# Half of the tokens by gathered expert rows, and GpSimd making lo parts: one encoder layer on one core

## The chip, the cores and the metric

The kernel runs on one core of a Trainium2 chip. The core has TensorE (PE, matrix products into PSUM), VectorE (DVE), ScalarE (ACT), GpSimd (POOL) and SyncE (SP, which here only issues DMAs). The metric is device microseconds of the program; the median of three runs counts. A profile is one more execution, taken by the hardware profiler.

## The reference, cut to what matters

One encoder layer on 1024 tokens of width 1024. The first half of it (gated linear attention, pooling, an output projection) is the same in both kernels. The second half is a product-key mixture of 16384 single-neuron experts:

```python
q = (ht @ w_q).reshape(T, 8, 2, 128)                       # 8 heads, two halves
s = einsum('thpd,hpnd->thpn', q, sub_keys)                 # 128 scores a half
vals, idx = top_k(s, 16)                                   # 16 best of each half
cand = vals[:, :, 0, :, None] + vals[:, :, 1, None, :]     # 256 sums
top_s, top_pos = top_k(cand.reshape(T, 8, 256), 16)        # 16 best sums: the chosen experts
gates = softmax(top_s)
a = gelu(einsum('td,ted->te', x, u_tab[experts]))          # 128 experts a token
y = einsum('te,ted->td', gates * a, v_tab[experts])
```

## The kernel before, in words

**Arithmetic.** Products in float32r keep float32's exactness by splitting each operand into a rounded part (`hi`, made by ScalarE, `split_hi`) and the rest (`lo`, a subtraction, `split_lo`). A product is then three matmuls: hi·hi, hi·lo, lo·hi. A "row" of experts is 128 x 1024 values (512 KB), and there are 128 such rows of u and of v.

**Tokens.** The 1024 tokens are 8 tiles of 128. Six are dense: the activation of every expert is computed and multiplied with a gate that is zero for the experts not chosen. Two are sparse (`SPARSE = 2`): for each of a token's 128 chosen experts GpSimd gathers the activation (`picked_act`, 4 bytes a token) and the row of v (`v_rows`, 4 KB a token) by indirect DMA, and VectorE adds the row, scaled, to a sum (`add_row`).

**Sweep 1** (`expert_sweep_1`) goes over the 128 rows of u. For each, TensorE makes 48 matmuls of 512 columns (8 slices of the width, 3 products, 2 halves of the tokens), ScalarE takes the gelu, and it goes to DRAM. Beside it VectorE finds the experts of the tokens, head by head (`topk_head`), and builds one-hot matrices of the chosen sub-keys by comparisons (`compare`, L1479); GpSimd multiplies these with the gates (L1393); and TensorE turns 8 tokens at a time into dense gates (L1555), which ScalarE copies and VectorE completes (L1492). VectorE also makes `u_lo` (L83).

**Sweep 2** (`expert_sweep_2`) goes twice over the 128 rows of v, three dense tiles a round (L1881: 18 matmuls a row and round). For each row VectorE multiplies gates and activations (`cf`, L1762), makes `c_lo` and `v_lo` (L83) and adds one gathered row (L1784). GpSimd issues the gathers in blocks of eight activations (L1668) and then eight rows (L1676), a row only when the sum that used its buffer is done.

The order on each engine is the order of the code; semaphores join the engines. TensorE's own loops are short, and each engine waits where its operands are not there.

Of the kernel before, what the change touches and what calls it, by code (L numbers as in the profile page):

```python
# [28 lines left out]
P = 128  # L29
D = 1024  # L30
# [18 lines left out]
TOK = 16  # L49
GTOK = P // 2  # L50
BLOCK_STEPS = GTOK // TOK
LOWEST = -3.0e38
SPARSE = 2
DENSE = TT - SPARSE
DTOK = DENSE * P
CHOSEN = HEADS * TOPK
TILE_STEPS = HEADS + 1
STEPS = NKEYS // 2
assert DENSE * TILE_STEPS + HEADS + 2 == STEPS
# [44 lines left out]
def layer(nc, t_in, out):  # L104
    g = Layer(nc, t_in, out)
    with ExitStack() as ctx:
# [44 lines left out]
        expert_sweep_1(g)  # L151
        expert_sweep_2(g)
# [856 lines left out]
def topk_buffers(g):  # L1009
    g.s_work = g.at("s_work", 96, [P, 2, NKEYS])  # L1010
    g.s_rest = g.at("s_rest", 97, [P, 2, NKEYS])
    g.cand = g.at("cand", 98, [P, TOPK, TOPK])
    g.cand_rest = g.at("cand_rest", 99, [P, TOPK, TOPK])
    g.match = g.at("match", 100, [P, 2, TOPK, TOPK])
    g.chosen = g.at("chosen", 102, [P, 2, HEADS, TOPK])
    g.top_all = g.at("top_all", 103, [P, HEADS, TOPK])
    g.vals = g.at("vals", 103.5, [P, 2, TOPK])
    g.tops = g.at("tops", 103.625, [P, TOPK])
    g.idx = g.at("idx", 103.6875, [P, 2, TOPK], U32)
    g.pos = g.at("pos", 103.8125, [P, TOPK], U32)  # L1020
    g.hilo = g.at("hilo", 103.875, [P, 2, TOPK], U32)
    g.gates = g.at("gates", 192, [P, HEADS, TOPK])
    g.norm = g.at("norm", 192.5, [P, HEADS])
    g.gate_hi = g.at("gate_hi", 194.75, [P, P], F32R)
    g.slots = g.at("slots", 192.75, [P, 4, P])


def topk_head(g, dve, h, topk_done):

    flat = lambda a: a.rearrange("p a b -> p (a b)")  # L1030
    for p in range(2):
        dve.max(g.vals[:, p, 0:8], g.s_work[:, p, :])
    dve.drain()
    for p in range(2):
        dve.max_index(g.idx[:, p, 0:8], g.vals[:, p, 0:8], g.s_work[:, p, :])
        dve.match_replace(g.s_rest[:, p, :], g.vals[:, p, 0:8], g.s_work[:, p, :], LOWEST)
# [4 lines left out]
    for p in range(2):  # L1041
        dve.max_index(g.idx[:, p, 8:16], g.vals[:, p, 8:16], g.s_rest[:, p, :])
# [912 lines left out]
```

## Time and profile before

| | us |
|---|---|
| runs (3) | 3346.50, 3348.01, 3355.24; median 3348.01 |
| profiled execution | 3326.69, its span 3324.8 |
| TensorE busy | 3126.2 (94% of the span), mean clock 0.978 |
| VectorE, ScalarE, GpSimd busy | 2256.7, 1017.1, 982.8 |
| HBM | 505.76 MB read, 134.22 MB written |

The span runs from the first instruction to the last. "Busy" of TensorE counts a matmul from start to its modelled end, so the pace of matmuls is read from their starts. The clock is what was granted, 1.00 being 2.4 GHz.

### The profile page before, as it was taken

How to read it: one execution, taken by the hardware profiler on the slowest of the kernel's cores; microseconds unless marked ns; L12 is line 12 of the kernel's file. 1: busy time of each engine (PE TensorE's matmuls, PEld its weight loads, DVE VectorE, ACT ScalarE, POOL GpSimd, SP SyncE). 2: the span in 40 equal slices, each digit the busy share in tenths (PEclk: the TensorE clock that was granted, in tenths of full speed). 3: DMA queues.
4: the chain of work that ended last, by engine and by line, in shares of the span. 5: the costliest groups of instructions: out<-in, count | busy, mean ns of one | idle time of the engine just before them, and what ended most of it. 6: DMA issues, size and time to landing. Idle time of an engine off the chain costs nothing. (4 is left out here: it accounts for less than half of the span.)

```text
span 3324.8 us, 44749 instructions
## 1 busy us (share of the span) xinstructions
PE 3126.2 (94%) x14706; PEld 2587.2 (78%) x14706; DVE 2256.7 (68%) x3986; ACT 1017.1 (31%) x1301; POOL 982.8 (30%) x727
## 2 busy tenths in 40 slices
PE   3993799989999999999999999999989998999996
PEld 3881587878888888888888888878878886788885
DVE  6345643568767677675876754438878888888886
ACT  3123453112232222322222221123333334333333
POOL 0000100013223233232332320026554557655541
PEclk9995899999999999999999999999999999999998
DMA  6410122223333423333233432249999999999995
GB/s 239 184 52 8 53 101 100 81 74 120 114 149 139 155 88 150 137 150 138 100 143 144 150 137 106 101 160 375 348 365 331 361 344 332 379 347 363 345 362 186
DMA packets 251408, 640.90 MB, mean 193 GB/s; under 512 B 28752, under 2 KB 134352, under 8 KB 249680
## 3 DMA queue, kind: packets, MB, share of 16 engines
q1 hardware_dynamic: 205568, 503.07, 41.2%
q0 software_dynamic: 45776, 137.00, 11.0%
q8 instruction: 37, 0.61, 0.1%
q14 instruction: 27, 0.22, 0.0%
HBM read 505.76 MB, written 134.22 MB: 192 GB/s over the span
## 5 line engine op out<-in xcount | busy, mean ns | idle before, releaser
L1393 POOL TENSOR_TENSOR onehot<-onehot,slots 128x1024 fp32r<-128x1024 f32 x192 | 369.1, 1944 | 1177.3 <-DVE onehot L1479 1177.3
L93 PE MATMUL acc_u<-a_hi,u_hi 128*128 128x512 f32 x2048 | 633.2, 390 | 2.5 <-PEq L1114 2.5
L93 PE MATMUL acc_u<-a_lo,u_hi 128*128 128x512 f32 x2048 | 631.2, 389 | 0.0
L93 PE MATMUL acc_u<-a_hi,u_lo 128*128 128x512 f32 x2048 | 630.8, 389 | 0.0
L1881 PE MATMUL y_ps<-v_hi,c_hi 128*128 128x512 f32 x1536 | 476.0, 391 | 31.4 <-DVE c_lo L83 29.1
L1881 PE MATMUL y_ps<-v_lo,c_hi 128*128 128x512 f32 x1536 | 474.6, 390 | 0.0
L1881 PE MATMUL y_ps<-v_hi,c_lo 128*128 128x512 f32 x1536 | 474.1, 390 | 0.0
L78 ACT ACTIVATE v_hi<-v_raw 128x1024 fp32r<-128x1024 f32 x256 | 271.5, 1061 | 649.1 <-PE y_ps L1881 619.1
L93 PEld LDWEIGHTS acc_u<-a_lo,u_hi 128*128 128x128 f32 x2048 | 384.6, 188 | 81.2
L93 PEld LDWEIGHTS acc_u<-a_hi,u_lo 128*128 128x128 f32 x2048 | 384.4, 188 | 80.5
L1415 ACT ACTIVATE gelu<-acc_u 128x1024 f32<-128x1024 f32 x128 | 131.5, 1027 | 1012.3 <-PE acc_u L93 1012.3
L93 PEld LDWEIGHTS acc_u<-a_hi,u_hi 128*128 128x128 f32 x2048 | 378.1, 188 | 75.2 <-issue 2.6
L83 DVE TENSOR_TENSOR v_lo<-v_raw,v_hi 128x1024 fp32r<-128x1024 f32 x256 | 314.4, 1228 | 172.1 <-ACT v_hi L78 171.7
L1676 POOL DMA_INDIRECT v_rows<-in_v,eidx x256 | 272.7, 1065 | 376.8 <-DVE y_part L1784 336.0
L1881 PEld LDWEIGHTS y_ps<-v_hi,c_hi 128*128 128x128 f32 x1536 | 288.1, 189 | 97.3 <-DVE v_lo L83 33.3
L1881 PEld LDWEIGHTS y_ps<-v_hi,c_lo 128*128 128x128 f32 x1536 | 289.1, 188 | 60.6
L1881 PEld LDWEIGHTS y_ps<-v_lo,c_hi 128*128 128x128 f32 x1536 | 289.1, 188 | 60.5
L1784 DVE SCALAR_TENSOR_TENSOR y_part<-v_rows,coef,y_part 128x1024 f32<-128x1024 f32 x256 | 331.4, 1297 | 0.1
L1668 POOL DMA_INDIRECT picked_act<-act_d,aidx x256 | 304.0, 1187 | 77.9 <-issue 77.9
L83 DVE TENSOR_TENSOR u_lo<-u_raw,u_hi 128x1024 fp32r<-128x1024 f32 x128 | 165.4, 1292 | 207.2 <-ACT u_hi L78 207.2
L1492 DVE TENSOR_TENSOR gate_block<-gate_block,gate_ps 128x1024 f32 (+1 forms) x96 | 116.7, 1216 | 214.4 <-ACT gate_block L1426 214.4
L1479 DVE TENSOR_TENSOR onehot<-consts,slots 128x1024 fp32r<-128x1024 f32 x192 | 239.4, 1288 | 0.9 <-issue 0.9
(227 smaller groups left out, 3403.9 us busy)
## 6 DMA issues: line engine op xcount, KB each, us to landing
v_raw<-in_v SPq DMA_DIRECT2D x256, 512.0 KB, 7.5
u_raw<-in_u SPq DMA_DIRECT2D x128, 512.0 KB, 4.2
act_d<-gelu SPq DMA_DIRECT2D x128, 512.0 KB, 2.6
gate_d<-gate_block SPq DMA_DIRECT2D x12, 4096.0 KB, 12.1
gt<-gate_d SPq DMA_DIRECT2D x64, 768.0 KB, 7.8
at<-act_d SPq DMA_DIRECT2D x256, 192.0 KB, 6.1
w_mod_b<-in_w_mod SPq DMA_DIRECT2D x6, 2560.0 KB, 9.0
w_mod<-in_w_mod SPq DMA_DIRECT2D x9, 1024.0 KB, 16.4
```

The lines of the kernel that those rows point to most:

```text
L78: return act.activation(hi, raw, ACT.Copy)
L83: return dve.tensor_tensor(lo, raw, hi.bitcast(F32), ALU.subtract)
L93: done = pe.matmul(acc[:, cols], w, a[:, k, cols], start=first, stop=last)
L1393: last_op = pool.tensor_tensor(onehot_2[u][:, :, part, :], onehot_2[u][:, :, 0, :].bitcast(F32), gate.unsqueeze(2).to_broadcast([P, TOK // ...
L1415: act.activation(gelu[s][:], acc[s][:], ACT.Gelu).then_inc(gelu_done, 1)
L1479: last = dve.tensor_tensor(rows, g.iota.unsqueeze(1).to_broadcast([P, TOK // 2, NKEYS]), chosen.unsqueeze(2).to_broadcast([P, TOK // 2, NK ...
L1492: dve.tensor_tensor(dst, dst, gate_psum(1), ALU.add).then_inc(gate_out, 1)
L1668: pool.indirect_dma_start(out=picked_act[:, e:e + 1], out_offset=None, in_=act_table, in_offset=bass.IndirectOffsetOnAxis(ap=index(g.aidx, ...
L1676: pool.indirect_dma_start(out=rows[e % UNROLL][:], out_offset=None, in_=v_table, in_offset=bass.IndirectOffsetOnAxis(ap=index(g.eidx, e), ...
L1784: dve.scalar_tensor_tensor(sums, rows[k][:], coef[:, k:k + 1], sums, ALU.mult, ALU.add).then_inc(rows_done, 1)
L1881: done = pe.matmul(yps[t][:, cols], c, v[s][:, cols], start=first and k == 0, stop=last and k == 2)
```

## The change

`SPARSE` goes from 2 to 4: four tiles are dense and four gathered. The experts' part becomes one program of three passes with one ring of four buffers for rows of u and v:

- pass 1: all rows of u against the sparse half of the tokens (24 matmuls a row). In it the retrieval and the dense gates are made, one head and eight tokens for each two rows. GpSimd makes `u_lo`.
- pass 2: all rows of u once more, against the dense half. VectorE makes `u_lo`. The gathers begin here: `rows_after` says how many rows are to be added after each row of experts, 7 for 3 rows, 284 in this pass.
- pass 3: all rows of v once, all four dense tiles (24 matmuls a row), with 23 gathered rows for 12 rows of experts, 228 in this pass. `cf`, `c_hi` and `c_lo` are made for two rows of experts at once, in one buffer of 128 x 1024.

Retrieval takes 112 candidate sums in place of 256 (with both lists sorted, the other 144 cannot be among the best 16), made by two small additions, and finds the experts of four heads at once (`decode_half`). The number of heads for which this is done in the experts' part stays 57. All engines' programs but TensorE's are written out without loops. GpSimd's gathers now alternate, one row and one activation, eight rows of either ahead. Dense gates are stored in blocks of 32 tokens in place of 64.

```diff
-SPARSE = 2
+WIDE = 4
+CANDS = WIDE * TOPK + (TOPK - WIDE) * WIDE
+SPARSE = 4
+GATE_TOK = 8
+ORDER = (1, 4, 2, 5, 3, 6, 7)
+FIRST_ROWS = 5
+def rows_after(x):
+    in_sweep_1 = max(0, min(x, 2 * HALF // 8 - 1) - FIRST_ROWS) * 7 // 3
+    return min(SPARSE * CHOSEN, in_sweep_1 + max(0, x - (2 * HALF // 8 - 1)) * 23 // 12)
...
+def half_product(pe, acc, w_hi, w_lo, a_hi, a_lo, half):
+    cols = slice(half * HALF, (half + 1) * HALF)
+    for k in range(KC):
+        wh, wl = w_hi[:, k * P:(k + 1) * P], w_lo[:, k * P:(k + 1) * P]
+        pe.matmul(acc, wh, a_hi[:, k, cols], start=k == 0, stop=False)
+        pe.matmul(acc, wh, a_lo[:, k, cols], start=False, stop=False)
+        done = pe.matmul(acc, wl, a_hi[:, k, cols], start=False, stop=k == KC - 1)
...
+            for p in range(U // 2):                                  # GpSimd, pass 1
+                split(2 * p + 2)
+                split(2 * p + 3)
+                if p:
+                    weigh(p - 1)
+            weigh(U // 2 - 1)
...
+            for r in range(BATCH):
+                pick_act(r)
...
+            for r in range(SPARSE * CHOSEN):                         # GpSimd, passes 2 and 3
+                fetch_row(r)
+                if r + BATCH < SPARSE * CHOSEN:
+                    pick_act(r + BATCH)
...
+            for p in range(U // 2):                                  # VectorE, pass 1
+                if p == 1:
+                    close(0)
...
+                    topk_head(g, dve, h, g.s_work[p % 2], topk_read)
+                    if h % HALF_HEADS == HALF_HEADS - 1:
+                        decode_half(g, dve, h // HALF_HEADS, g.chosen[n % 2])
...
+                    compare(p - 1)
+                if p >= 2:
+                    gates_low(p - 2)
...
+                for half in range(2):                                # VectorE, pass 2
+                    split(e + 2 + half)
+                    upto = rows_after(2 * p + half)
+                    for r in range(done, upto):
+                        add_row(r)
...
+            for m in range(N_STEPS):                                 # VectorE, pass 3
+                if m % 2 == 0 and m + 2 < N_STEPS:
+                    combined(m // 2 + 1)
+                if m + 2 < N_STEPS:
+                    split(V + m + 2)
+                upto = rows_after(U + m)
+                for r in range(done, upto):
+                    add_row(r)
...
+                if m % 2 == 0 and m + 2 < N_STEPS:
+                    combined_low(m // 2 + 1)
```

GpSimd in the u sweep, before: one step of 16 tokens, four multiplications with the gates and no lo part (`onehot_3592` and `onehot_3593` are the two buffers of one-hot matrices).

```order
L1393 TENSOR_TENSOR onehot_3592<-onehot_3592,slots 128x8x128
L1393 ISA
L1393 TENSOR_TENSOR onehot_3592<-onehot_3592,slots 128x8x128
L1389 REGISTER_ALU
L1393 ISA
L1393 TENSOR_TENSOR onehot_3593<-onehot_3593,slots 128x8x128
L1393 ISA
L1393 TENSOR_TENSOR onehot_3593<-onehot_3593,slots 128x8x128
```

In pass 1 of the changed kernel, two pairs of rows of u:

```order
L99 TENSOR_TENSOR u_lo_3799<-u_raw_3795,u_hi_3797 128x1024
L99 TENSOR_TENSOR u_lo_3800<-u_raw_3796,u_hi_3798 128x1024
L1457 TENSOR_TENSOR onehot_3804<-onehot_3804,slots 128x8x128 x2
L99 TENSOR_TENSOR u_lo_3057<-u_raw_3053,u_hi_3055 128x1024
L99 TENSOR_TENSOR u_lo_3058<-u_raw_3054,u_hi_3056 128x1024
L1457 TENSOR_TENSOR onehot_3803<-onehot_3803,slots 128x8x128 x2
```

Each pair of rows now puts two subtractions and two multiplications in GpSimd's queue.

VectorE in the u sweep, before, from the middle of one head's retrieval to the end of its step:

```order
L1043 TENSOR_TENSOR cand<-vals 128x256
L1047 MAX tops<-cand 128x8
L1049 MAX_INDEX pos<-tops,cand 128x8
L1050 MATCH_REPLACE cand_rest<-tops,cand 128x256
L1052 MAX tops<-cand_rest 128x8
L1054 MAX_INDEX pos<-tops,cand_rest 128x8
L1055 ISA
L1055 COPY top_all<-tops 128x16
L1058 TENSOR_SCALAR hilo<-pos 128x16
L1059 TENSOR_SCALAR hilo<-pos 128x16
L1062 TENSOR_TENSOR match<-hilo,consts 128x512
L1065 TENSOR_TENSOR match<-match,idx 128x512
```

In pass 1 of the changed kernel the same stretch, up to the next head:

```order
L1061 TENSOR_TENSOR cand<-vals 128x64
L1064 TENSOR_TENSOR cand<-vals 128x48
L1069 MAX top_all<-cand 128x8
L1071 MAX_INDEX pos<-top_all,cand 128x8
L1072 MATCH_REPLACE cand_rest<-top_all,cand 128x112
L1074 MAX top_all<-cand_rest 128x8
L1076 MAX_INDEX pos<-top_all,cand_rest 128x8
L1611 TENSOR_TENSOR onehot_3801<-consts,slots 128x1024
L1611 TENSOR_TENSOR onehot_3803<-consts,slots 128x8x128
L1618 TENSOR_TENSOR gate_block_3805<-gate_block_3805,ps 128x128x8
```

The one addition has become two next to each other, and the search for the experts has left the head's step.

GpSimd's gathers, before: a block of eight activations, and rows (`v_rows_7646` and so on are the eight buffers).

```order
L1668 DMA picked_act<-act_d,aidx 128x1 x8
L1676 DMA v_rows_7646<-in_v,eidx 128x1024
L1676 DMA v_rows_7647<-in_v,eidx 128x1024
L1676 DMA v_rows_7648<-in_v,eidx 128x1024
L1676 DMA v_rows_7649<-in_v,eidx 128x1024
```

And in the changed kernel:

```order
L1487 DMA v_rows_3816<-in_v,eidx 128x1024
L1479 DMA picked_act<-act_s,aidx 128x1
L1487 DMA v_rows_3817<-in_v,eidx 128x1024
L1479 DMA picked_act<-act_s,aidx 128x1
L1487 DMA v_rows_3818<-in_v,eidx 128x1024
```

There are still two gathers for each row of v, now one behind the other, and twice as many in all.

## Rows read from the trace of the kernel before

**Rows 1.** Stages: start:end, length, PE, PEld, DVE, ACT, POOL busy (count), clock, DMA share, GB/s.

```profile
520.00:700.00 180.00, 179.70 (x906) 152.66 (x905) 82.39 (x229) 30.61 (x31) 0.00 (x0) 1.00 0.27 91
743.00:2200.00 1457.00, 1453.25 (x6761) 1217.04 (x6762) 976.70 (x2177) 388.66 (x385) 359.69 (x188) 1.00 0.35 130
2221.00:2740.00 519.00, 507.56 (x2221) 419.66 (x2222) 410.48 (x503) 183.01 (x247) 286.40 (x262) 0.98 0.95 349
3298.00:3325.00 27.00, 0.97 (x5) 0.47 (x3) 10.75 (x11) 5.33 (x12) 5.83 (x4) 0.59 0.24 97
```

**Rows 2.** First matmuls of the u sweep, by tile (duration min/median/max; first, last start).

```profile
L93 PE MATMUL acc_u<-a_hi,u_hi x2048: 389/389/628, 716.5 to 2213.0; 128*128 128x512 f32 x187
```

**Rows 3.** PE in order of time, 1007 to 1020 us (start, duration, what).

```profile
1007.52 1.12 PE L1555 MATMUL gate_ps<-onehot,onehot 128*128 128x256 f32 x8
1008.47 0.63 PE L93 MATMUL acc_u<-a_hi,u_hi 128*128 128x512 f32 x2
...
1019.38 1.12 PE L1555 MATMUL gate_ps<-onehot,onehot 128*128 128x256 f32 x8
```

**Rows 4.** VectorE in order of time from 717 us, GpSimd idle.

```profile
717.27 0.49 DVE L1032 MAX8 vals<-s_work 128x8 f32<-128x128 f32 x2
...
720.14 0.41 DVE L1043 TENSOR_TENSOR cand<-vals 128x256 f32<-128x256 f32 x1
...
725.46 0.69 DVE L1067 TENSOR_REDUCE chosen<-match 128x32 f32<-128x512 f32 x1
```

**Rows 5.** VectorE in order of time, 1017 to 1028 us.

```profile
1017.32 1.43 DVE L1043 TENSOR_TENSOR cand<-vals 128x256 f32<-128x256 f32 x1
1018.82 0.43 DVE L1047 MAX8 tops<-cand 128x8 f32<-128x256 f32 x1
...
1021.19 0.16 DVE L1055 COPY top_all<-tops 128x16 f32 x1
...
1023.96 1.21 DVE L1492 TENSOR_TENSOR gate_block<-gate_block,gate_ps 128x1024 f32 x1
...
1026.23 2.35 DVE L1479 TENSOR_TENSOR onehot<-consts,slots 128x1024 fp32r<-128x1024 f32 x2
```

**Rows 6.** GpSimd over the same stretch.

```profile
1014.71 3.76 POOL L1393 TENSOR_TENSOR onehot<-onehot,slots 128x1024 fp32r<-128x1024 f32 x2 [5.89 <-DVE onehot L1479]
```

**Rows 7.** VectorE, the same operation without and with a GpSimd operation beside it.

```profile
401.15 1.23 DVE L83 TENSOR_TENSOR wo_lo<-wo_raw,wo_hi 128x1024 fp32r<-128x1024 f32 x1 [2.55 <-ACT wo_hi L78]
...
403.49 2.20 DVE L83 TENSOR_TENSOR wo_lo<-wo_raw,wo_hi 128x1024 fp32r<-128x1024 f32 x1
```

**Rows 8.** GpSimd there, and its add in the tail.

```profile
402.15 12.48 POOL L83 TENSOR_TENSOR a_lo<-z,a_hi 128x1024 fp32r<-128x1024 f32 x4 [85.19 <-ACT a_hi L78]
...
3312.08 2.33 POOL L1683 TENSOR_TENSOR y<-y,x 128x1024 f32<-128x1024 f32 x1 [5.68 <-DVE y L1796]
```

**Rows 9.** Groups by line, sweep 2 (count, busy us, mean ns, idle before).

```profile
L1784 DVE SCALAR_TENSOR_TENSOR y_part<-v_rows,coef,y_part 128x1024 f32<-128x1024 f32 x256 | 331.4, 1297 | 0.1
...
L1668 POOL DMA_INDIRECT picked_act<-act_d,aidx x256 | 304.0, 1187 | 77.9 <-issue 77.9
...
L1676 POOL DMA_INDIRECT v_rows<-in_v,eidx x256 | 272.7, 1065 | 376.8 <-DVE y_part L1784 336.0 <-issue 40.8
```

**Rows 10.** GpSimd gathers in order of time at 2318 us.

```profile
2318.32 1.67 POOL L1668 DMA_INDIRECT picked_act<-act_d,aidx  x1 [0.30 <-issue]
2320.29 1.36 POOL L1668 DMA_INDIRECT picked_act<-act_d,aidx  x1 [0.30 <-issue]
2321.95 0.94 POOL L1668 DMA_INDIRECT picked_act<-act_d,aidx  x1 [0.30 <-issue]
```

**Rows 11.** VectorE over the same stretch.

```profile
2319.08 0.55 DVE L83 TENSOR_TENSOR c_lo<-cf,c_hi 128x384 fp32r<-128x384 f32 x1
...
2320.74 0.55 DVE L1762 TENSOR_TENSOR cf<-gt,at 128x384 f32<-128x384 f32 x1
2322.07 1.23 DVE L83 TENSOR_TENSOR v_lo<-v_raw,v_hi 128x1024 fp32r<-128x1024 f32 x1 [0.78 <-ACT v_hi L78]
```

More of the change, by code:

```diff
@@ L1020, in topk_buffers @@
[L1020 to L1030, printed above, removed]
+    g.s_work = [g.at(f"s_work{s}", 88 + s, [P, 2, NKEYS]) for s in range(2)]
+    g.match = g.at("match", 90, [P, 2, HALF_HEADS * TOPK, TOPK])
@@ new lines, in fetch_row @@
+            def fetch_row(r):
+                if r >= ROWS:
+                    pool.wait_ge(rows_done, r - ROWS + 1)
+                pool.indirect_dma_start(out=rows[r % ROWS][:], out_offset=None, in_=v_table,
+                                        in_offset=bass.IndirectOffsetOnAxis(ap=index(g.eidx, r), axis=0))\
+                    .then_inc(rows_in[r % ROWS], 16)
+            pool.wait_ge(aidx_ready, 1)
+            for s in range(2):
+                pool.wait_ge(act_stored[s], U // 2 * 16)
@@ new lines, in gates, with pair @@
+            def gates(b, u, first=False):
+                pe.wait_ge(onehot_ready, b + 1)
+                if not first:
+                    pe.wait_ge(gate_out, b)
+                for t in range(GATE_TOK):
+                    last = pe.matmul(gps[:, t], onehot_1[u][:, t, :], onehot_2[u][:, t], start=True, stop=True)
+                last.then_inc(gate_ps, 1)
+            def pair(p, odd, half=1, first_gates=False, slots=None):
+                e = 2 * p
+                pe.wait_ge(lo_pool, e + 1)
+                product(e, 2 * odd, 1)
+                gates(p - 2, odd, first_gates)
+                if slots is not None:
+                    transpose_slots(slots)
+                pe.wait_ge(lo_pool, e + 2)
+                product(e + 1, 2 * odd + 1, 1)
@@ new lines, in _ @@
+            for e in range(4):
+                pe.wait_ge(lo_pool, e + 1)
+                product(e, e, 1, e >= 2)
+                if e == 2:
+                    transpose_slots(0)
+            pair(2, 0, first_gates=True)
+            pair(3, 1)
+            for j in range(DENSE):
+                first = TILE_GATES * j + (4 if j == 0 else 2)
+                with pe.Fori(first // 2, TILE_GATES * (j + 1) // 2) as q:
+                    pair(2 * q, 0)
+                    pair(2 * q + 1, 1)
+                if j + 1 < DENSE:
+                    pair(TILE_GATES * (j + 1), 0)
+                    pair(TILE_GATES * (j + 1) + 1, 1, slots=j + 1)
@@ L1901, in lay_out @@
+            for s in range(RING):
+                m = N_STEPS - RING + s
+                if s % 2 == 0:
+                    pe.wait_ge(clo_r, m // 2 + 1)
+                combine(V + m, s, last=s == RING - 1)
 def lay_out(a):
```

1063 lines of the change are left out of this document (482 added, 581 removed).

## The prediction

> **What bounds the kernel now.** I read the stages first, then each engine in order of time. In the u sweep TensorE is busy for 1453.25 of 1457 us, in a round of the v sweep for 507.56 of 519 [rows 1]: its matmuls set the time. The sweep's first matmul starts at 716.5 us [rows 2]. 48 matmuls lie between 1008.47 and 1019.38: 10.91 us, 0.227 us each; eight gate matmuls take 0.95 us [rows 3]. VectorE and GpSimd have room, but the DMA engines in the v sweep show a share of 0.95 at 349 GB/s.
>
> **How VectorE and GpSimd meet.** An addition of two 256-element inputs takes 0.41 us alone and 1.43 us when it is issued inside two GpSimd operations that run from 1014.71 to 1018.47; it ends at 1018.75 [rows 4 to 6]. A VectorE subtraction of 1.23 us takes 2.20 us in the 12.48 us in which GpSimd makes four subtractions (3.12 us each, 2.33 us for one with less beside it) [rows 7, 8]. So an operation of one with both inputs in SBUF waits for the other's to end, and they take turns. The gathers show it too: the one issued at 2318.32 takes 1.67 us and the next VectorE operation starts at 2319.08; that of 2320.29 takes 1.36, VectorE's next starts at 2320.74; that of 2321.95 finds VectorE idle and takes 0.94 [rows 10, 11]. Each is 0.9 us after the end of VectorE's current operation. Two issued in a row have 0.3 us between them (2320.29 + 1.36 to 2321.95).
>
> **Up to 716.5 us: no change.** TensorE is busy for 179.70 of 180 us in the retrieval stage [rows 1]; the shorter top-k hides behind it. Cost 0.
>
> **Pass 1 (before: 1498 us from 716.5 to about 2214).** TensorE needs 10.91 + 0.95 = 11.86 us for a pair of rows, 64 pairs: 759 us. VectorE's sum for a pair with a head:
> - top-k up to the candidates 2.87 (717.27 to 720.14) [rows 4], two additions 0.4, the rest 2.37 before (1018.82 to 1021.19) [rows 5], less 0.8 because 112 elements in place of 256 shorten five operations by some 0.16: with drains 4.9;
> - two comparisons 2.35 and the gates' sum 1.2 [rows 5]; 0.3 for semaphores, my estimate;
> - the search for four heads at once: three operations of 2048 elements; 512 take 0.69 [rows 4] and 1024 take 1.2 [rows 7], so about 2.3 each, with the small ones 7.7, a quarter of it 1.9; the close of a tile 0.3 a pair.
> That is 10.9 us, under 11.86. But GpSimd has two subtractions of about 2.3 and two multiplications of 1.88 (3.76 for two [rows 6]): 8.4 us. They begin when VectorE's comparison ends, since the multiplications wait for it, and the subtractions' inputs are there already. The candidates are asked for 4.1 us later, after the gates' sum and 2.87 of top-k; GpSimd's first subtraction ends at about 6.1. The first addition waits 2.1 us. The second finds GpSimd's second subtraction at the door: a whole turn of 2.2 us, or nothing if the 0.2 us of the first is too short for GpSimd to ask. I take the middle, 1.1. Pair: 14.1 us, VectorE's, and TensorE waits for the one-hot matrices. 57 such pairs are 804 us; some 6.5 more without a head are TensorE's, 77. Pass 1: 881 (bounds: 759 with all waits hidden, 945 with two whole turns; wholly serial, 57 x (10.9 + 8.4) + 77 = 1177, is excluded since the searches and MAX operations of VectorE run beside GpSimd in rows 5 and 6).
>
> **Pass 2.** TensorE: 128 x 24 x 0.227 = 698 us. VectorE: one subtraction of 1.2 and 2.33 rows of 1.2 (its mean 1.297 [rows 9]) are 4 to 4.3 of 5.45 us a row of experts: enough. GpSimd: a gathered row costs two gathers. Means 1187 and 1065 ns with 0.3 us between issues [rows 9] make 2.85; leaving out that a row which waited for VectorE is a little cheaper, 2.9. Beside less VectorE work in this pass I take 2.87. 7/3 rows a row of experts are then 6.7 us against 5.45: GpSimd becomes the bound, VectorE waits for the rows in its queue, behind that wait stand the subtractions for the next rows of u, and TensorE waits for these. The gathers start when the last gates are stored and eight activations are fetched, some 25 us in. 25 + 284 x 2.87 = 840 us. Bounds: 2 x 1.24 = 2.48 a row if no gather ever waits (0.94 [rows 10] and 0.3), 729 us; 3.3 a row if half of VectorE's operations are met at their start, 962.
>
> **Pass 3.** TensorE again 698 us. VectorE for two rows of experts: two subtractions 2.4, 3.83 rows 4.7, `cf` and `c_lo` 2.3, together 9.5 of 10.9. It has more operations that a gather can meet, so 3.0 us a row: 228 x 3.0 = 684, then nine rows of experts without gathers, 49, and 15 us for late transfers: 748 us (bounds 698 and, at 3.3, 816). Before, two rounds took 1077 us.
>
> **DMA.** Pass 2 moves 67 MB of u, 34 MB of activations out, 149 MB of rows: 250 MB in 840 us, 298 GB/s. Pass 3: 67 MB of v, 120 of rows, 67 of gates and activations, 6 of x and results: 260 MB in 748 us, 348 GB/s, what the v sweep carries now at 0.95 [rows 1]. It hides just so; that is what the 15 us are for. Gates now come in pieces of 512 bytes, which no row prices: between 0 and 60 us, I take 0 beyond the 15.
>
> **Clock.** In the tail, where TensorE has nearly stopped, the granted clock is 0.59 between the levels 1.2 and 2.4 GHz; in the sweeps it is 1.00 and 0.98 [rows 1]. TensorE will pause for 2 of 14 us in pass 1 and up to 10 us in the 15 pairs with a search. If each of these lets the clock fall for one product, 5.45 us become 10.9, 15 x 5.45 = 82 us; I take 0, because TensorE leads there and VectorE sets the pace.
>
> **Tail.** 27 us before [rows 1]; GpSimd's adds of 2.33 [rows 8] become VectorE's of 1.2, and one tile more is to be finished: 20. Written-out programs must be fetched as they run; the four engines' words are few beside 250 MB: 0.
>
> **Sum.** 716 + 881 + 840 + 748 + 20 = 3205 us of span; the profiled execution before has 3324.8, and 3326.69 with what lies around it. Its median is 1.0064 times that, so 3207 x 1.0064 = **3227 us**, 3.6% less than 3348. The matmuls that go (1536 in the v sweep, 348 us, and 256 of the gates, 30 us) are worth 378 us by themselves; the new bounds on VectorE and GpSimd give 260 of it back.
>
> **A rule against this sum.** Rows 10 and 11 show gathers waiting for VectorE operations with two SBUF inputs. The Trainium skill, page "SBUF — State Buffer", section "Who interferes with whom", says that such an operation takes only the read side of the shared ports and that writing DMA descriptors needs the write side (it marks this as inferred), so that it doesn't delay a GpSimd DMA. By that rule only the first rival below would be left of this cost.
>
> **Rivals.**
> - *The gathers don't wait* (2.48 us a row; perhaps the index is read early once row and activation alternate). Pass 2 729, pass 3 713: 3059 of span, 3080. For it: many gathers of 0.94. Against: means of 1.07 and 1.19 [rows 9]. This is the page's rule as well.
> - *VectorE and GpSimd slip past each other in pass 1*, which then runs at TensorE's 11.86 to 12.1 us a pair: 770 us, 3094 of span, 3115. For it: 10.9 is under 11.86. Against: GpSimd's turns in rows 7 and 8. With the first rival too: 2950, 2970.
> - *Slower than before: every gather is held for most of a VectorE operation.* Rows of 1.2 us stand back to back, and 1.24 us of gather just misses each end; at 3.4 us a row both passes are 25 + 512 x 3.4 + 64 = 1830, with two whole turns in pass 1 (945): 3511 of span, 3533. It decides from 3.24 us a row (with pass 1 as forecast). For it: the 1.67 us gather. Against: the mean over 512 gathers.
> - *The DMA engines bind pass 3*, by pieces of 512 bytes: 60 us more, 3290. For it: 0.95 already.
>
> **Numbers.** Forecast 0.45, its own range 3130 to 3300; gathers that don't wait 0.12; pass 1 hidden 0.15; both 0.06; slower 0.12; DMA 0.10. Below 3338 (0.3% under 3348, about what a measurement tells from no change) lie all but the slower case and some 0.03 of the rest: faster 0.85, within 0.3% 0.03, slower 0.12. The range of 8 in 10 is 3040 to 3350: it holds all single rivals but the slower one, and leaves out both together.
>
> **What would show it.** Pass 1: the span between the starts of TensorE's first products of two pairs, 14.1 us with a head and 11.86 after the last; `cand` of VectorE above 2 us for the first addition; TensorE's gate matmuls waiting for GpSimd's `onehot`. Pass 2: GpSimd without idle time but 0.3 us, 2.87 us from row to row; VectorE's longest wait on the DMA of `v_rows`, TensorE's on `u_lo`. Pass 3: the same at 3.0, DMA share at 0.95. The forecast is wrong if TensorE is over 97% busy in pass 1 or pass 2, if rows follow each other in under 2.5 us or over 3.2, or if the head of the kernel moves by over 5 us.

## The result: 0.5% slower, and the profile after

The changed kernel takes 3366.62 us (median of 5 runs, 3361.34 to 3373.39) against 3348.01 us: ratio 1.0048, 95% interval 1.0032 to 1.0065. The forecast was 3227 us, so it was wrong in size and in sign. The profiled execution takes 3365.42 us, its span 3363.6 us.

The stages of the changed kernel, first the answer to [rows 1]: start:end, length, busy us of each engine (count), granted clock, DMA share, GB/s. The second row is pass 1's first 864 us, the third goes from the first row gather to the first matmul of the v sweep, the fourth to the last one.

```profile
520.00:700.00 180.00, 176.20 (x874) 149.16 (x873) 70.86 (x206) 28.92 (x29) 0.00 (x0) 0.99 0.27 91
722.90:1587.00 864.10, 722.12 (x3212) 594.29 (x3212) 816.69 (x1835) 259.22 (x311) 475.01 (x224) 0.92 0.44 147
1699.40:2604.50 905.10, 751.04 (x2960) 585.56 (x2958) 494.54 (x448) 189.46 (x247) 622.93 (x571) 0.89 0.82 277
2604.50:3352.00 747.50, 719.29 (x3072) 582.10 (x3072) 587.83 (x525) 202.12 (x210) 538.56 (x446) 0.98 0.93 339
```

The marks of the stages in order of time: the first matmul of the u sweep (as [rows 2]), the first and the last row gather, and TensorE's last matmuls.

```profile
722.90 0.47 PE L1260 MATMUL ps<-a_hi,u_hi 128*128 128x512 f32 x1 [2.31 <-PEq L1151]
1699.43 0.96 POOL L1487 DMA_INDIRECT v_rows<-in_v,eidx  x1 [6.07 <-DMA gate_d<-gate_block]
3290.14 1.66 POOL L1487 DMA_INDIRECT v_rows<-in_v,eidx  x1 [0.30 <-issue]
3351.70 0.61 PE L1825 MATMUL ps<-u_hi,spare_lo 128*128 128x512 f32 x2
```

| us | forecast | measured | difference |
|---|---|---|---|
| to the first u matmul | 716.5 | 722.9 | +6.4 |
| pass 1 and the 25 us to the first row gather | 881 + 25 = 906 | 976.5 | +70.5 |
| pass 2 from there to the first v matmul | 815 | 905.1 | +90.1 |
| pass 3 | 748 | 747.5 | -0.5 |
| tail | 20 | 11.6 | -8.4 |
| span | 3205 | 3363.6 | +158.6 |

**Pass 1, VectorE and GpSimd.** VectorE's candidate additions (L1061, L1064), the comparisons behind them and the next head's first search for maxima, in order of time over one pair without a search; then GpSimd over the same stretch. They answer to [rows 5, 6].

```profile
876.30 2.36 DVE L1061 TENSOR_TENSOR cand<-vals 128x64 f32<-128x64 f32 x1
878.59 2.41 DVE L1064 TENSOR_TENSOR cand<-vals 128x48 f32<-128x48 f32 x1
882.86 2.36 DVE L1611 TENSOR_TENSOR onehot<-consts,slots 128x1024 fp32r<-128x1024 f32 x2
886.27 0.48 DVE L1049 MAX8 vals<-s_work 128x8 f32<-128x128 f32 x2
889.14 2.35 DVE L1061 TENSOR_TENSOR cand<-vals 128x64 f32<-128x64 f32 x1
```
```profile
876.18 4.75 POOL L99 TENSOR_TENSOR u_lo<-u_raw,u_hi 128x1024 fp32r<-128x1024 f32 x2
885.30 3.75 POOL L1457 TENSOR_TENSOR onehot<-onehot,slots 128x1024 fp32r<-128x1024 f32 x2 [4.38 <-DVE onehot L1611]
889.02 2.39 POOL L99 TENSOR_TENSOR u_lo<-u_raw,u_hi 128x1024 fp32r<-128x1024 f32 x1
```

The first addition is issued 0.1 us after GpSimd's subtraction has begun and lasts to its end; the second lasts as long as GpSimd's second. They have 64 and 48 elements a partition. The same two lines over all 57 heads (duration in ns min/median/max), and TensorE's waits in pass 1 (us in total, times, longest):

```profile
L1061 DVE TENSOR_TENSOR cand<-vals x57: 206/2352/2371, 725.8 to 1569.9; 128x64 f32<-128x64 f32 x57
L1064 DVE TENSOR_TENSOR cand<-vals x57: 201/2411/2424, 725.9 to 1572.2; 128x48 f32<-128x48 f32 x57
```
```profile
PE ps L1773 <- POOL onehot L1457: 143.0, 36, 9.3
```

From the first head's candidates to the 57th's are 1569.9 - 725.8 = 844.1 us, 15.07 a pair; a pair without search takes 889.14 - 876.30 = 12.84.

**Pass 2.** The waits from 1699.4 to 2604.5 us, the chain that ended last in that stretch (its shares and its longest piece), and GpSimd's gathers there and in pass 3 (the last two rows), which answer to [rows 9]:

```profile
ACT gelu L1515 <- PE ps L1262: 340.4, 66, 19.2
DVE u_lo L99 <- ACT u_hi L94: 286.3, 29, 20.0
ACT gelu L1515 <- remote: 285.1, 29, 23.6
...
POOL v_rows L1487 <- DVE y_part L1650: 93.3, 23, 8.1
```
```profile
by line: PE ps L1260 19.7%; PE ps L1262 19.4%; another core or an unknown queue 19.2%; PE ps L1261 18.9%; issue 13.5%; DMA act_d<-gelu 1.7%; ACT u_hi L94 1.5%; POOL v_rows L1487 1.3%; DVE y_odd L1650 1.2%; POOL picked_act L1479 1.0%; ACT ge
...
1724.03 23.53 another core or an unknown queue
```
```profile
L1487 POOL DMA_INDIRECT v_rows<-in_v,eidx x286 | 325.5, 1138 | 201.3 <-DVE y_part L1650 93.3 <-issue 77.1 <-DVE y_odd L1650 24.8
L1479 POOL DMA_INDIRECT picked_act<-act_s,aidx x285 | 298.1, 1046 | 86.9 <-issue 86.9
...
L1487 POOL DMA_INDIRECT v_rows<-in_v,eidx x227 | 273.7, 1206 | 82.3 <-issue 60.0 <-DVE y_part L1650 14.7 <-DVE y_odd L1650 7.6
L1479 POOL DMA_INDIRECT picked_act<-act_s,aidx x219 | 266.2, 1215 | 66.7 <-issue 66.7
```

GpSimd is not full: 93.3 + 24.8 us of its idle time wait for VectorE's additions of rows. VectorE stands at the `u_lo` subtraction, for ScalarE's `u_hi`; ScalarE stands at the gelu. I read what the profile calls "remote" and "an unknown queue" there as the landing of the gelu's store two tiles back: the code has no other wait at that place but the tile's matmuls. One such wait, ScalarE, SyncE's queue and GpSimd's last gather in order of time, and the busy times in its last stretch of 2 us (columns as in the table of stages):

```profile
1712.24 0.60 ACT L1515 ACTIVATE gelu<-ps 128x512 f32<-128x512 f32 x1 [3.24 <-PE ps L1262]
1721.54 0.60 ACT L1515 ACTIVATE gelu<-ps 128x512 f32<-128x512 f32 x1 [8.70 <-remote]
...
1747.58 1.09 ACT L1515 ACTIVATE gelu<-ps 128x512 f32<-128x512 f32 x2 [23.55 <-remote]
```
```profile
1712.87 0.33 SPq L1360 DMA_DIRECT2D act_d<-gelu  x1
1722.16 0.33 SPq L1360 DMA_DIRECT2D act_d<-gelu  x1
...
1748.20 0.81 SPq L1360 DMA_DIRECT2D act_d<-gelu  x2
```
```profile
1742.94 0.94 POOL L1479 DMA_INDIRECT picked_act<-act_s,aidx  x1 [0.30 <-issue]
```
```profile
1746.00:1748.00 2.00, 0.00 (x0) 0.00 (x0) 0.00 (x0) 0.42 (x1) 0.00 (x0) 0.50 0.02 6
```

The first gelu at 1747.58 needs the buffer of the gelu at 1712.24, whose store is issued at 1712.87. By that reading the store lands some 34 us after its issue; in the last 2 us the DMA engines move almost nothing, and still it has not landed. GpSimd's last gather before it ends at 1743.88, 3.7 us earlier. In the profiles of the changed kernel on A, C, D and E (the chips of the table below) there are 37 such waits of over 15 us, and 30 of them end 1.9 to 5.6 us after GpSimd has stopped. That suggests that a store lands when the gathers pause. It is not shown: GpSimd stops there because VectorE does, and VectorE because of the same wait.

TensorE loses time of its own in this pass. Its waits from 1699.4 to 2604.5 us, and its matmuls near the end of the tile before that wait:

```profile
PE ps L1260 <- issue: 64.8, 43, 9.1
PE ps L1260 <- ACT gelu L1515: 37.8, 10, 10.1
PE ps L1261 <- issue: 23.4, 30, 1.7
PE ps L1262 <- issue: 22.3, 24, 2.1
```
```profile
1738.43 0.58 PE L1261 MATMUL ps<-a_lo,u_hi 128*128 128x512 f32 x1 [0.80 <-issue]
1740.54 0.59 PE L1262 MATMUL ps<-a_hi,u_lo 128*128 128x512 f32 x1 [1.52 <-issue]
```

"Issue" is time in which an engine waited for nothing that the profile shows. Here it is 110.5 us of TensorE, and 45.7 of them (L1261, L1262) lie inside a tile, where the code has no wait. From 1724.44 to 1740.54 TensorE makes 15 matmuls in 16.1 us, which take 3.4 at 0.227 each.

### The profile page after: what moved, and what is told of

Same layout as the page of the kernel before. It is cut to its first block, busy times and chain, and to the rows that moved or that the text cites. A ratio compares the mean times of both kernels' runs of the same rounds, so it can differ in the third digit from the quotient of the medians.

```text
span 3363.6 us, 36366 instructions
## 1 busy us (share of the span) xinstructions
PE 2885.1 (86%) x12908; PEld 2327.6 (69%) x12908; DVE 2312.8 (69%) x3493; ACT 913.3 (27%) x1184; POOL 1733.5 (52%) x1289
## 4 chain that ended last, share of the span: by engine, by line
PE 33%; DVE 23%; issue 7%; another core or an unknown queue 5%; POOL 4%; DVEq 3%; DMA 2%; ACT 1%; SPq 0%; ACTq 0%
PE ps L1825 14%; PE ps L1260 6%; PE ps L1262 6%; PE ps L1261 6%; DVE cand L1064 4%; DVE cand L1061 4%; DVE onehot L1611 2%; POOL picked_act L1479 2%; POOL v_rows L1487 2%; DVEq L1050 2%; DVE gate_block L1618 2%; DMA v_rows<-in_v,eidx 1%; DVE idx L1059 1%; DVE match L1096 1%
## 5 line engine op out<-in xcount | busy, mean ns | idle before, releaser
L1260 PE MATMUL ps<-a_hi,u_hi 128*128 128x512 f32 x2048 | 833.0, 407 | 105.6 <-issue 64.8
L1261 PE MATMUL ps<-a_lo,u_hi 128*128 128x512 f32 x2048 | 827.2, 404 | 23.8 <-issue 23.4
L1262 PE MATMUL ps<-a_hi,u_lo 128*128 128x512 f32 x2048 | 824.7, 403 | 22.9 <-issue 22.3
L1479 POOL DMA_INDIRECT picked_act<-act_s,aidx x512 | 572.8, 1119 | 162.2 <-issue 155.8
L1825 PE MATMUL ps<-u_hi,spare_lo 128*128 128x512 f32 x2048 | 562.8, 395 | 24.6 <-issue 13.3
L1260 PEld LDWEIGHTS ps<-a_hi,u_hi 128*128 128x128 f32 x2048 | 402.7, 197 | 214.3 <-issue 90.3
L1261 PEld LDWEIGHTS ps<-a_lo,u_hi 128*128 128x128 f32 x2048 | 402.5, 197 | 118.0 <-issue 38.3
L1262 PEld LDWEIGHTS ps<-a_hi,u_lo 128*128 128x128 f32 x2048 | 401.3, 196 | 111.4 <-issue 26.3
L1825 PEld LDWEIGHTS ps<-u_hi,spare_lo 128*128 128x128 f32 x2048 | 388.2, 190 | 118.3 <-issue 38.7
L94 ACT ACTIVATE u_hi<-u_raw 128x1024 fp32r<-128x1024 f32 x384 | 389.1, 1051 | 169.1 <-PE ps L1825 107.3
```

The lines of the kernel that those rows point to most:

```text
L94: return act.activation(hi, raw, ACT.Copy)
L1260: pe.matmul(acc, wh, a_hi[:, k, cols], start=k == 0, stop=False)
L1261: pe.matmul(acc, wh, a_lo[:, k, cols], start=False, stop=False)
L1262: done = pe.matmul(acc, wl, a_hi[:, k, cols], start=False, stop=k == KC - 1)
L1479: pool.indirect_dma_start(out=picked_act[:, b % 4, r % BATCH:r % BATCH + 1], out_offset=None, in_=act_table, in_offset=bass.IndirectOffset ...
L1825: done = pe.matmul(yps[t][:, half, :], c, v[slot][:, out], start=first and n == 0, stop=last and n == 2)
```

## The experiments

I call the chip of the first result A; its number is not on record. The five behind it, B to F, are five different ones, and A may be one of them. Each row is one chip; pass 2 goes from the first row gather to the first v matmul in the profile of the changed kernel (on B, which did not run it, of the kernel with four gelu buffers).

| chip | before, us | changed, us | ratio | pass 2, us |
|---|---|---|---|---|
| A | 3348.0 | 3366.6 | 1.0048 (1.0032 to 1.0065) | 905 |
| B | 3329.4 | not run | | 819 |
| C | 3360.2 | 3384.8 | 1.0073 (1.0044 to 1.0102) | 913 |
| D | 3350.9 | 3367.9 | 1.0024 (0.9994 to 1.0054) | 912 |
| E, one run each | 3370.4 | 3407.3 | 1.011 | 938 |
| F, one run each | 3328.3 | 3283.6 | 0.987 | 813 |

Below, the chips with a pass 2 of 813 to 819 us (B, F) are the short kind, and those with 905 to 938 us (A, C, D, E) the long kind. "Kind of chip" is a name and not a cause: each chip of B to F was met in one series only, so nothing tells the chip from whatever else was the same throughout its series.

### Chip B: the two suspects

The theory: two separate causes, the additions' waits in pass 1 and the late stores in pass 2. The rival to each: it is only beside what bounds.

**lo parts on VectorE.** The two subtractions of a pair go back to VectorE, behind the top-k of the pair.

```
 # GpSimd, each pair of pass 1
-                split(2 * p + 2)
-                split(2 * p + 3)
 # VectorE, behind topk_head(...)
+                    split(2 * p + 2)
+                    split(2 * p + 3)
```

> In pass 1 VectorE makes all lo parts of u again, both of a pair right after the pair's top-k instructions; GpSimd keeps only the multiplications of the one-hots with the gates. All else as in the changed kernel. Theory (the candidate additions wait for GpSimd's whole subtractions): both additions fall back to about 0.2 us, a pair without search costs VectorE about 12.84 - 2 x 2.2 + 2.4 = 10.9 us, and pass 1 ends 100 to 120 us earlier, near 840 us; the time is about 3255 us. Rival (TensorE's clock or its queue bounds pass 1, the waits are only beside it): pass 1 stays above 930 us and the time within 20 us of 3366. Passes 2 and 3 do not move in either.

Measured: 3176.97 us, ratio 0.9548 (0.9532 to 0.9564). Pass 1 to the first row gather is 861.8 us in place of 976.5, 115 less, inside the expectation. The additions again (duration ns min/median/max):

```profile
L1061 DVE TENSOR_TENSOR cand<-vals x57: 202/205/1129, 725.3 to 1458.7; 128x64 f32<-128x64 f32 x57
L1064 DVE TENSOR_TENSOR cand<-vals x57: 194/201/205, 725.5 to 1458.8; 128x48 f32<-128x48 f32 x57
```

Their waits were 2.15 + 2.21 = 4.36 us a pair, and the two subtractions cost VectorE 2 x 1.22 = 2.44; the difference, 1.92 x 57 = 109 us, is what the offload cost by this estimate. But pass 2, which the edit does not touch, was 815.8 us, 89 less than on chip A, and the time was 80 us below the expectation. That raised the question of the chips.

**Four gelu buffers** for the tiles 8 to 103 of pass 2.

```
-    gelu = [g.at(f"gelu{s}", 104 + 2 * s, [P, HALF]) for s in range(2)]
+    gelu = [g.at(f"gelu{s}", (104, 106, 100, 102)[s], [P, HALF]) for s in range(4)]
+    gelu_of = lambda e: e % 4 if U + 8 <= e < U + 104 else e % 2
```

> In pass 2 four gelu buffers in place of two for nearly all tiles, so that a gelu waits for the landing of the store four tiles back and not two. Pass 1 as in the changed kernel. Theory (the landing of the stores, 10 to 23 us, binds pass 2 beside the gathers): ScalarE's waits on the stores, 285 us in pass 2, fall below 60 us; pass 2 falls from 910 us towards the price of GpSimd's gathers, 800 to 850 us; the time is 3270 to 3310 us. Rival (GpSimd's gathers bind pass 2 and the store waits only fill the slack): ScalarE's waits fall too, pass 2 stays within 15 us of 910 and the time within 15 us of 3366, or the gathers now left over run into pass 3.

Measured: 3293.36 us, ratio 0.9887 (0.9871 to 0.9904); pass 2 819.3. ScalarE's waits for stores fell to 92 us there, not below 60. It looked like the theory's confirmation and was not: 819 us is what this chip gives without the edit too (815.8 above), and the runs on D below show that it gains nothing.

**Both edits.**

> The two edits together: VectorE makes all lo parts in pass 1, and four gelu buffers in pass 2. If the two causes are separate stages, the gains add: 3366 less the gain of the one and the gain of the other, 3155 to 3200 us by the theory, which is below the kernel before (3348). If the gathers bind from the end of pass 1 to the last row whatever TensorE does in pass 2, the time is that of the first edit alone, about 3255 us.

Measured: 3171.38 us, ratio 0.953; pass 1 861.7, pass 2 818.0. The second edit adds nothing to the first here.

**Seven of eight activation gathers left out**, after the first four batches.

```
-                if r + BATCH < SPARSE * CHOSEN:
+                if r + BATCH < SPARSE * CHOSEN and (r + BATCH < 4 * BATCH or r % BATCH == 0):
                     pick_act(r + BATCH)
```

> Leaves out the gathers of seven of eight activations after the first four batches (the coefficients are then made of old numbers): GpSimd issues about half as many gathers, and the row gathers, their bytes and VectorE's additions stay. Theory with GpSimd's issue as the bound of passes 2 and 3: a row costs 1.13 + 0.3 us in place of about 2.8, so the last row comes in pass 2's time or early in pass 3, and TensorE is free of VectorE's additions later. If the store landings bind pass 2 and not the gathers: pass 2 still takes 850 us or more, since the rows' bytes now come at twice the rate and ScalarE's waits for the stores stay above 200 us. If the gathers bind: pass 2 falls to 760 us or less and the waits for the stores fall with it.

Measured: 3091.55 us (one run); pass 2 677.5, pass 3 697, what TensorE's matmuls need. So with all gathers these are the bound of both passes on this chip; without most of them it is TensorE (672.7 of 677.5 us busy), with the DMA engines at 0.98.

### Chip C: the control, and how the transfers are issued

> The changed kernel itself, run once more, beside the runs that follow. In the changed kernel's first profile pass 2 took 905 us, while with the lo parts back on VectorE in pass 1, where pass 2's own code is untouched, it took 816 us. Theory A (the 905 us belong to the program: the rhythm in which it enters pass 2 makes the gelu stores land late): pass 2 is 895 to 915 us again and the ratio to the kernel before is 1.003 to 1.007 again. Theory B (they belong to that chip or that execution): pass 2 is about 816 us, the ratio 0.975 to 0.985, and the first edit of the first series then gained only pass 1's 115 us.

Measured: ratio 1.0073, pass 2 913.3: neither theory is refuted, since C is like A (the kernel before takes 3360 us here, not 3329).

**The subtractions in pieces.**

```
-                split_lo(pool, lo[e % RING][:], raw[e % RING][:], hi[e % RING][:]).then_inc(lo_pool, 1)
+                for c in range(0, D, D // 4):
+                    last = split_lo(pool, lo[e % RING][:, c:c + D // 4], raw[e % RING][:, c:c + D // 4],
+                                    hi[e % RING][:, c:c + D // 4])
+                last.then_inc(lo_pool, 1)
```

> GpSimd still makes all lo parts of pass 1, but each subtraction in four of 256 columns in place of one of 1024. Theory (a candidate addition waits until the one GpSimd instruction that is running has ended): the two waits fall from 2.35 and 2.41 us to 0.6 to 0.9 us each, a pair without search from 12.84 us towards 11.9 us or less, and pass 1 from 976 us to 880 to 930 us. Rival (VectorE waits until GpSimd has no instruction ready, however short each is): the additions take as long as before or longer, 4 us and more since two subtractions follow one another, and pass 1 stays at 976 us or grows.

Measured: 3315.16 us, ratio 0.987 (0.9845 to 0.9896); pass 1 882.0 us, pass 2 920.8. The additions, and GpSimd's pieces:

```profile
L1061 DVE TENSOR_TENSOR cand<-vals x57: 205/1175/1889, 726.9 to 1476.8; 128x64 f32<-128x64 f32 x57
L1064 DVE TENSOR_TENSOR cand<-vals x57: 192/751/769, 727.1 to 1477.8; 128x48 f32<-128x48 f32 x57
...
L99 POOL TENSOR_TENSOR u_lo<-u_raw,u_hi x512: 722/742/2792, 729.7 to 1572.5; 128x256 fp32r<-128x256 f32 x171
```

The second addition takes one piece's time, 0.75 for 0.74 us. So the wait is for the end of the running instruction, and after one VectorE instruction GpSimd gets the next turn. The first addition's 1.18 is above the 0.9 expected. Most of the loss of pass 1 is back with the work still on GpSimd.

**Four rows in flight, not eight** (`ROWS = 4`).

> Four row gathers in flight at most in place of eight. Pass 1 does not move. If the gelu stores land late because eight rows' bytes are queued ahead of them, the stores land in half the time, ScalarE's waits for them fall, and pass 2 falls by 40 us or more from the control's. If the stores are not the bound of pass 2: no gain there, and where GpSimd waits for VectorE's additions to free a row (four rows are 11.4 us of gathers), pass 2 and pass 3 grow, together by 0 to 150 us.

Measured: 3389.34 us, ratio 1.0095 (1.0069 to 1.0121), the control's within the spread. Pass 2 fell to 865.8 us, 47 less, which is over the 40 us that the first theory asked for, and pass 3 grew from 759 to 792: given back, most of it. ScalarE's longest wait for a store fell from 24.2 to 17.5 us, but the sum of these waits did not fall (401 us against 406 on the control, "remote" and "DMA act_d" together), and nothing shows the stores landing in half the time. Fewer gathers in flight make the long pass 2 shorter; whether by their bytes or their number this run cannot tell.

**Stores on ScalarE's queue.**

```
+                if e >= U:
+                    act.wait_ge(gelu_done, e + 1)
+                    act.dma_start(g.act_d[e - U], gelu[e % 2][:]).then_inc(act_stored[e % 2], 16)
```

> In pass 2 the gelu stores are issued on ScalarE's queue right behind each gelu, not on SyncE's behind the waits for the lo parts and the loads of u. Theory (the landing counts from an issue that SyncE makes late, since the store of a pair's even tile stands behind the second lo): the waits of ScalarE for its stores fall by half or more, and pass 2 falls from the control's value by 30 us or more, down to GpSimd's price of about 810 us. Rival (GpSimd's gathers bind, the store waits only fill its slack): pass 2 stays within 10 us of the control's.

Measured: 3421.06 us (3380.46 to 3430.3), ratio 1.0149 (1.0075 to 1.0224), pass 2 937.0, where the theory wanted 30 us less than the control's 913. ScalarE's "remote" waits stay (364 us for 374). The theory falls: SyncE's late issue is not the cause. Why the edit costs 24 us more was not studied.

### Chip D: the edits against the control on one chip

> The changed kernel again, now on one chip with the two edits of the first series. So far pass 2 took 905 and 913 us where the kernel before took 3348 and 3360 us, and 816 to 819 us, in edited kernels, where it took 3329 us. If these are two kinds of chip, all kernels of this series have the same kind of pass 2: with the kernel before near 3329 us the control's pass 2 is about 820 us and its time about 3285 us (ratio 0.985); with it at 3348 us or more, 905 us and a ratio of 1.003 to 1.008.

> The lo parts of pass 1 on VectorE, as in the first series, on the chip of the control. Pass 1 is 110 to 120 us below the control's by either theory. If the kind of chip sets pass 2, pass 2 equals the control's within 15 us and the time is 105 to 135 us below the control's. If the program sets it, pass 2 is about 816 us while the control's is 905 or more, and the time is some 200 us below.

> Four gelu buffers in pass 2, on the chip of the control. On a chip of the kind with 905 us: if the late stores are the cause, pass 2 falls by 50 us or more; if the buffers are no cause, it stays within 15 us of the control's. On a chip of the kind with 816 us: no change beyond 10 us, since GpSimd's gathers set pass 2 there.

> Both edits, on the chip of the control: the sum of what the two gain alone in this series, within 20 us. On a chip of the 905 us kind with the late stores as a cause that is 160 us or more below the control; on one of the 816 us kind 105 to 130 us.

Measured: 3367.92 us the control, 3255.24 with the lo parts on VectorE (ratio to before 0.9723, 0.969 to 0.9755), 3368.22 with four buffers (1.0037), 3253.13 with both (0.9699, 0.9671 to 0.9728), 115 us below the control, the sum of the two. Moving the lo parts back is worth 113 us by the medians, what pass 1 gives (861.4 against 976.8). Pass 2 is 881.8 us there, 912.0 in the control and 903.7 with both edits: over the 15 us that was allowed, but the control's own executions lie 45 us apart, and the profiled one of the first edit was its fastest (3236.33). Four buffers are worth 0: pass 2 is 23 us shorter (888.7), between the two limits that were set, and pass 3 18 us longer. ScalarE's waits for stores in the kernel with four, 1720 to 2590 us:

```profile
ACT gelu L1520 <- remote: 353.5, 38, 27.5
```

The control has 338.0, 29, 24.2 over the same stretch. With twice the buffers the waits are no shorter: what makes a store late makes the next ones late too.

### Chip E: which transfer

The stores with 32 of 512 columns in pass 2 (pass 1 writes `act_d` whole instead); the rows with 256 of 1024 columns, all but the first eight; and the activation gathers left out as on B:

```
+                    sp.dma_start(g.act_d[e - U][:, 0:32], gelu[e % 2][:, 0:32]).then_inc(act_stored[e % 2], 16)
```
```
+                pool.indirect_dma_start(out=rows[r % ROWS][:] if wide else rows[r % ROWS][:, 0:D // 4],
+                                        out_offset=None, in_=v_table if wide else v_quarters,
```

> The changed kernel on the chip of this series. Pass 2 is 905 to 915 us on a chip of the slow kind, 815 to 820 us on one of the other kind; the next three are read against it.

> Pass 2's gelu stores carry 32 of 512 columns (act_d is written whole in pass 1, a second store of each tile, so pass 3 reads old activations). If the stores' bytes or their place behind other bytes bind pass 2 on the slow kind of chip, pass 2 falls from 910 us to 840 us or less and ScalarE's waits for stores below 100 us. If any transfer comes late there, whatever it is, pass 2 falls by less than 30 us. On the fast kind no change over 15 us.

> All row gathers after the first eight fetch 256 of 1024 columns (the rest of each row stays that of an earlier one): as many gathers, a quarter of their bytes. If the rows' bytes ahead in the DMA engines make the stores late, pass 2 falls to GpSimd's price, 284 x 2.6 to 2.85 us = 740 to 810 us, on both kinds of chip, and the DMA share of pass 2 falls below 0.6. If the number of gathers is the cause, pass 2 stays within 20 us of the control's.

> Seven of eight activation gathers left out after the first four batches, as in the first series, where pass 2 took 678 us with the DMA engines 99% busy on the fast kind of chip. If GpSimd's issue is what binds on both kinds, 680 to 740 us here too. If the slow kind is slow in moving the bytes, pass 2 stays above 800 us here.

One run each. Pass 2 of the four, in this order (columns as in the table of stages):

```profile
1699.40:2637.30 937.90, 768.75 (x2959) 591.87 (x2957) 494.39 (x447) 189.25 (x247) 616.33 (x580) 0.87 0.80 270
```
```profile
1699.00:2600.50 901.50, 745.15 (x2961) 583.34 (x2959) 497.85 (x448) 189.21 (x246) 635.69 (x577) 0.89 0.77 247
```
```profile
1700.10:2620.80 920.70, 753.03 (x2957) 585.29 (x2956) 494.10 (x447) 189.12 (x246) 618.31 (x570) 0.88 0.49 154
```
```profile
1699.30:2394.10 694.80, 678.27 (x2959) 559.13 (x2958) 491.79 (x448) 190.18 (x246) 423.63 (x349) 0.99 0.97 363
```

Neither the stores' bytes nor the rows' matter much (36 and 17 us below the control's 938, which is itself above the 915 expected; executions on D differ by as much; the DMA share falls to 0.49 and the pass stays at 921). With the activation gathers mostly gone the two kinds of chip come within 17 us of each other: 694.8 here, 677.5 on B, although the bytes now come at 363 GB/s. TensorE's time in "issue" goes with them, from 141.9 us in the control to 10.9. So what a chip of the long kind loses hangs on the activation gathers and not on bytes. Whether it is their number or that they fetch single elements no run separates.

### Chip F: the changed kernel on a chip of the short kind

The second kernel stores no activations in pass 2 (pass 1 writes them to both places):

```
                 if e < U:
                     sp.dma_start(g.act_s[e], gelu[e % 2][:]).then_inc(act_stored[e % 2], 16)
+                    sp.dma_start(g.act_d[e], gelu[e % 2][:]).then_inc(act_stored[e % 2], 16)
```

> The changed kernel on the chip of this series: pass 2 of 905 to 940 us on the slow kind, 815 to 820 us on the other.

> Pass 2 stores no activations (pass 1 writes them to both places, pass 3 reads old ones), so no gelu of pass 2 waits for a landing; all 1024 gathers stay. If the late stores are the only way by which pass 2 is lengthened: pass 2 falls to GpSimd's price, 284 rows x 2.78 to 2.87 us plus 25 = 815 to 840 us, on the slow kind of chip too. If the gathered activations and rows are themselves late there, VectorE waits for them and pass 2 stays above 870 us.

Measured, one run each: 3283.55 us the changed kernel (before: 3328.29) and 3285.55 without the stores; pass 2 813.1 and 819.2. Here the unedited change has the short pass 2, so the program alone does not cause the long one. The waits (the last two lines are TensorE's, all it has) and the gathers of the changed kernel in pass 2, and the chain that ended last there:

```profile
ACT gelu L1515 <- DMA act_d<-gelu: 517.8, 74, 14.0
DVE y_part L1650 <- DMA v_rows<-in_v,eidx: 125.5, 72, 5.8
...
PE ps L1260 <- ACT gelu L1515: 55.6, 35, 4.5
PE ps L1260 <- DVE u_lo L99: 30.8, 22, 3.1
```
```profile
L1487 POOL DMA_INDIRECT v_rows<-in_v,eidx x286 | 320.4, 1120 | 93.2 <-issue 78.9 <-DMA gate_d<-gate_block 6.3 <-DVE y_part L1650 4.0
L1479 POOL DMA_INDIRECT picked_act<-act_s,aidx x285 | 319.5, 1121 | 86.8 <-issue 86.8
```
```profile
by line: POOL v_rows L1487 24.8%; POOL picked_act L1479 24.7%; DMA v_rows<-in_v,eidx 20.5%; issue 20.3%; DVE y_odd L1650 2.6%; DVE y_part L1650 2.4%; DVE u_lo L99 1.1%; DMA picked_act<-act_s,aidx 0.9%; PE ps L1262 0.8%; PE ps L1260 0.7%; PE
```

ScalarE waits for stores even more in total, 518 us against 285, but never over 14 us at once, and taking all these waits away changes nothing: GpSimd's gathers bind. The sum of waits was the wrong number to look at; their longest, and whose they are in the chain, told the two kinds apart.

The sharpest mark is another one. TensorE has no "issue" time at all in pass 2 on B and F, in any of the kernels there, and 110.5, 137.3, 126.9 and 141.9 us in the changed kernel on A, C, D and E. And it waits for ScalarE's gelu less on A (37.8 us) than on F (55.6). So the late stores are one sign of what happens on the long kind and cannot be called its cause. Something that the profile does not show holds TensorE too. An obvious candidate, that instructions reach the engines late, was not tested. As this pair of runs landed on the short kind, it could not tell by what way the long kind is slow.

## Why the prediction was wrong

- **To 716.5 us:** taken as 0, it was 6.4 us, more than the 5 that the forecast named as a sign of being wrong. TensorE is busy for 176.20 of 180 us in the retrieval stage, where it was 179.70. Not studied further.
- **Pass 1, the step that failed first.** The mechanism was right: VectorE's additions wait for GpSimd's turns, TensorE for `onehot` (143 us). "The second finds GpSimd's second subtraction at the door: a whole turn of 2.2 us, or nothing ... I take the middle, 1.1": it is the whole turn, 2.41 - 0.20 = 2.21 us. The 57 pairs took 15.07 us each, not 14.1: 55 of the 70 us. The other 15 lie behind the last head; one wait of TensorE for `onehot`, 9.2 us before 1591.3, is in them, and the rest was not taken apart. The stated bound, 945, left them out too. A bound that is one event with two outcomes has no middle: GpSimd's two subtractions stand back to back, so here the second addition loses a whole turn. The pieces on C and the undoing on B and D show it (977 to 882 and to 862 us). One argument of the forecast had no row that showed it, that VectorE's MAX operations run beside GpSimd; the line of 886.27 does, 0.48 us for two beside GpSimd's multiplication.
- **Pass 2, the step that failed second.** "GpSimd becomes the bound" at 2.87 us a row, 815 us behind the first 25. On F it took 813.1 (a row 1.120 + 1.121 + 0.61 = 2.85) and on B 816 to 819. On A, C, D and E it took 905 to 938, on A 3.19 us a row: GpSimd is not the bound there. In the waits shown above GpSimd stands for VectorE, VectorE for ScalarE, ScalarE for a store that lands some 34 us after its issue, and TensorE stands 110.5 us for nothing that the profile shows. The forecast put both at nothing: it has no term for a store's landing or for stops of TensorE inside a tile, and the fetching of the written-out programs, which might have to do with the stops, it put at 0. What is behind both stays open. Bounds of 729 to 962, with the first 25 us in them, held A's 930.
- **Pass 3:** right, 747.5 for 748, rows at (3290.14 - 2604.5) / 227 = 3.02 us for 3.0. The same gathers run there without stores, and with the changed kernel's own gathers it was nowhere longer than 772 us.
- **DMA and clock:** 0.93 at 339 GB/s in pass 3, as said, and the rival of 60 us more did not come. The clock in pass 1 is 0.92 and, on A, 0.89 in pass 2 against 0.96 on F; TensorE's busy time there is 751 against 714 us, so part of the long pass 2 is products at the lower clock, for which the forecast took 0.
- **Tail:** 11.6 for 20 us.
- **The rivals.** That gathers don't wait fell: their means are 1.12 and 1.12 us on F, 1.05 to 1.22 on A, over the 0.94 of one that meets nothing. The Trainium skill's rule in "SBUF — State Buffer", section "Who interferes with whom", by which VectorE would not delay them, is not borne out by these rows. The slower rival had two mechanisms; its "two whole turns" came true, its 3.4 us a row did not. Its limit was worked out wrongly: with pass 1 as forecast the sum 716 + 881 + 25 + 512 x + 64 + 20 reaches the 3324.8 of before at x = 3.16 us a row, not 3.24.

With pass 1's turn priced whole (945) and the rest as forecast the sum would be 3269 us of span and 3292 of time, and chip F shows 3283.6. So pass 1's error alone would have left the change 1.7% faster; the sign turned with the 90 us of pass 2, which the forecast had no ground to expect from its rows and whose cause is not known.

**The better version.** The changed kernel with the lo parts on VectorE beats the kernel before, ratio 0.9548 (0.9532 to 0.9564) on B and 0.9723 (0.969 to 0.9755) on D, and on D the changed one too (3255.24 for 3367.92 us).

## What to carry to other kernels

In this kernel, work on two SBUF inputs that moved from VectorE to GpSimd cost VectorE a whole GpSimd instruction for each of its own small ones that met it: count these meetings, not busy time. Here 4.36 us of waits bought 2.44 us of work. If the work must stay on GpSimd, cut it in shorter instructions. And before an improvement is read from an edit, run the unedited kernel on the same chip: four buffers looked like 2% on B (3293 us beside the 3367 of A) and were nothing.

## What had not been expected of the hardware

- The same program differs from chip to chip, or from series to series: the kernel before by 1% (3328 and 3329 against 3348 to 3370 us), the changed one by 2.5 to 3.8% (3284, one run, against 3367 to 3407), nearly all in pass 2 (813 against 905 to 938 us).
- On the long kind a store of 256 KB lands some 34 us after its issue while 128-element gathers are in flight, with a DMA share of 0.02 in the last 2 us, and TensorE stands 110 to 142 us in pass 2 for nothing that the profile shows, 0 on the short kind. Stores of a sixteenth of the bytes are hardly better; without seven of eight single-element gathers the long waits and the stops are nearly gone. By what way these gathers act stays open, and whether the landings or TensorE's own stops carry the loss: the kernel without stores was not seen on such a chip.
- A VectorE addition of 48 elements a partition takes 0.20 us alone and 2.41 us beside GpSimd's subtractions of 1024.
